# Seven half-width products in place of eight for the SwiGLU down projection, with the weight sums made by GpSimd

## What is computed

```python
def swiglu(h, w_gate_up, w_down):
    g, u = jnp.split(h @ w_gate_up, 2, axis=-1)
    return (jax.nn.silu(g) * u) @ w_down

        x = x + rms_norm(ca, g_mem_post[l])
        h = rms_norm(x, g_ffn_pre[l])
        x = x + rms_norm(swiglu(h, w_gate_up[l], w_down[l]), g_ffn_post[l])
```

## Time and profile before

| | |
|---|---|
| three runs | 1463.42, 1463.74, 1464.24 us, median 1463.74 |
| profiled execution, its own time | 1463.54 us |
| its span in the profile | 1461.7 us |
| PE busy | 1449.6 us (99%) |
| DVE, ACT, POOL busy | 897.9, 616.6, 242.0 us |
| granted clock of PE, mean | 1.000 |

### The profile page before, as it was taken

One profiled execution on the slowest core, in us unless ns is written; L12 is line 12 of the kernel. 1 busy time (PEld: TensorE's weight loads), 2 busy tenths in 40 slices (PEclk: granted clock), 3 DMA queues, 4 the chain that ended last, 5 costly groups with the idle time before them and its releaser, 6 DMA issues.

```text
span 1461.7 us, 21937 instructions
## 1 busy us (share of the span) xinstructions
PE 1449.6 (99%) x8234; PEld 1208.5 (83%) x8234; DVE 897.9 (61%) x1389; ACT 616.6 (42%) x960; POOL 242.0 (17%) x215
## 2 busy tenths in 40 slices
PE   9999999999999999999999899999999999999999
PEld 6888779898899888888888688888888888888787
DVE  6524673566638655455323787747666866767878
ACT  6222775453345222223223542334665433334654
POOL 0200102020020000000000565545522110110000
PEclk9999999999999999999999999999999999999999
DMA  5622103422023665754422122232203333334643
GB/s 177 202 87 93 53 2 122 138 87 87 1 87 116 204 186 185 223 175 155 166 86 90 55 87 90 96 103 87 60 2 87 87 91 110 86 98 132 223 152 122
DMA packets 159251, 164.06 MB, mean 112 GB/s; under 512 B 7357, under 2 KB 134589, under 8 KB 157765
## 3 DMA queue, kind: packets, MB, share of 16 engines
q1 hardware_dynamic: 157268, 159.84, 34.5%
...
q10 hardware_dynamic: 1056, 0.00, 0.0%
...
## 4 chain that ended last, share of the span: by engine, by line
PE 96%; DVE 2%; POOL 1%; DMA 0%; ACT 0%; issue 0%; SPq 0%; DVEq 0%; ACTq 0%; POOLq 0%
PE ps L2259 27%; PE ps L2261 27%; PE ps L2260 27%; PE ps L2696 3%; PE ps L2785 1%; PE ps L2803 1%; PE ps L2886 1%; PE ps L2895 1%; PE ps L2706 1%; PE ps L547 1%; POOL x_t L863 1%; DVE w_lo L2169 1%; DMA raw<-in_w_in 0%; PE ps L2727 0%; PE ps L2954 0%; PE ps L2955 0%
## 5 line engine op out<-in xcount | busy, mean ns | idle before, releaser
L2259 PE MATMUL ps<-a_hi,w_hi 128*128 128x512 f32 (+2 forms) x1576 | 588.6, 373 | 4.9 <-POOL w_lo L811 2.3
L2261 PE MATMUL ps<-a_hi,w_lo 128*128 128x512 f32 (+2 forms) x1576 | 583.3, 370 | 0.0
L2260 PE MATMUL ps<-a_lo,w_hi 128*128 128x512 f32 (+2 forms) x1576 | 583.0, 370 | 0.0
L2259 PEld LDWEIGHTS ps<-a_hi,w_hi 128*128 128x128 f32 (+1 forms) x1576 | 296.2, 188 | 61.3 <-DVE a_lo L1626 4.2
L2261 PEld LDWEIGHTS ps<-a_hi,w_lo 128*128 128x128 f32 (+1 forms) x1576 | 296.2, 188 | 51.6
L2260 PEld LDWEIGHTS ps<-a_lo,w_hi 128*128 128x128 f32 (+1 forms) x1576 | 296.3, 188 | 50.9 <-issue 0.7
L949 ACT ACTIVATE w_hi<-raw 128x2048 fp32r<-128x2048 f32 x105 | 200.8, 1913 | 254.6 <-PE ps L2261 240.2
L1511 DVE TENSOR_TENSOR w_lo<-raw,w_hi 128x2048 fp32r<-128x2048 f32 x85 | 194.6, 2289 | 154.2 <-ACT w_hi L949 153.7
L811 POOL TENSOR_TENSOR w_lo<-raw,w_hi 128x2048 fp32r<-128x2048 f32 x22 | 101.4, 4608 | 435.7 <-ACT w_hi L949 408.0
L2017 DVE TENSOR_TENSOR arena<-ps,rstd 128x512 f32<-128x512 f32 x88 | 59.8, 687 | 137.6 <-PE ps L2261 132.6
L2259 PE MATMUL ps<-w_hi,a_hi 128*128 128x512 f32 x346 | 135.6, 392 | 1.3 <-DVE w_lo L2169 0.9
...
## 6 DMA issues: line engine op xcount, KB each, us to landing
raw<-in_w_gate_up SPq DMA_DIRECT2D x44, 512.0 KB, 5.6
raw<-in_ffn_w_up SPq DMA_DIRECT2D x44, 512.0 KB, 4.7
raw<-in_attn_w_in SPq DMA_DIRECT2D x36, 512.0 KB, 4.5
raw<-in_w_in SPq DMA_DIRECT2D x24, 512.0 KB, 4.7
arena<-in_ffn_w_down SPq DMA_DIRECT2D x24, 512.0 KB, 4.1
...
raw<-in_w_down SPq DMA_DIRECT2D x22, 512.0 KB, 4.4
raw<-in_w_mem_kv SPq DMA_DIRECT2D x16, 512.0 KB, 4.4
```

Source lines behind the costliest of these rows:

```text
L2259: pe.matmul(dst, s_hi, m_hi, start=start, stop=False, skip_group_check=across)
L2260: pe.matmul(dst, s_hi, m_lo, start=False, stop=False, skip_group_check=across)
L2261: return pe.matmul(dst, s_lo, m_hi, start=False, stop=stop, skip_group_check=across)
```

## The change

`ffn_down` becomes seven products of blocks. Both the contraction (each pair of row tiles: rows k=0 and k=1) and the features (two halves of 512) and the tokens (two halves of 256) are cut in two, and seven products of sums of quarters replace eight. Tokens move, 256 at a time. There are 29 steps. Eleven (`DownStep`, one for each pair) hold four of the seven products, with 4 x 4 x 3 = 48 matmuls of 256 tokens. Eighteen (`SingleStep`) are three runs of six steps, each run one product: five steps of two pairs (24 matmuls) and one step of one pair (12 matmuls). The four products share PSUM banks with the single ones: a result is copied out by ACT (`staged_quarter`) or added by DVE (`join_down`) before the run that goes on in its bank.

Weight quarters are summed by POOL, not by DVE: for each of eleven pairs it loads the two row tiles, makes four sums of 128x512, and stores four quarters to `sums_1_dram`. The steps of `ffn_down` read one quarter from `w_down` and three from there, in a ring of four buffers. The sums of activation quarters are POOL's `basis` (two of 128x256 for each pair, as the hidden tiles get ready), three more for a pair are DVE's (`sides`, `fourth_side`). Squares are taken of quarters of the result in the steps 15, 20 and 26 and at the end; the gain moves from ACT's copy into DVE's scaling (L1644 and L1638 become `scalar_tensor_tensor`).

The core of the diff ("..." where lines are left out):

```diff
-    ("ffn_up", 22, 2, 2, "dve"), ("ffn_down", 11, 1, 0, ""),
+    ("ffn_up", 22, 2, 2, "dve"), ("ffn_down", 29, 1, 0, ""),
...
+                self.run, m = (c - PAIRS_K) // 6, (c - PAIRS_K) % 6
+                self.pairs = range(2 * m, min(2 * m + 2, PAIRS_K))
+                self.many = len(self.pairs)
+                self.opens, self.closes = m == 0, m == 5
...
+            def load_down():
+
+                for t in DOWNS:
+                    if t.c < 2:
+                        sp.wait_ge(weights_split, t.g + CREDIT - 1)
+                    elif t.c < 4:
+                        sp.wait_ge(hidden_written, CREDIT + FT)
+                    else:
+                        sp.wait_ge(weights_split, t.g + CREDIT - 3)
+                    if t.c == 0:
+                        sp.wait_ge(rel_moved, SUMS_1_MOVED + 48 * PAIRS_K)
+                    if t.first:
+                        sp.dma_start(t.q[:, 0, :], w_down_1[t.pair, 0][:, 0:512]).then_inc(t.landed, 16)
+                        sp.dma_start(t.q[:, 1:3, :], sums_1_dram[t.pair, :, 0:2, :]).then_inc(t.landed, 16)
+                        sp.dma_start(t.q[:, 3, :], sums_1_dram[t.pair, :, 3, :]).then_inc(t.landed, 16)
+                    else:
+                        def operand(pair):
...
+                                return sums_1_dram[pair, :, 2, :]
+                            return w_down_1[pair, 1].rearrange("p (q n) -> p q n", n=512)[:, 2 - t.run, :]
+                        if t.many == 2:
+                            for j, pair in enumerate(t.pairs):
+                                sp.dma_start(t.q[:, j, :], operand(pair)).then_inc(t.landed, 16)
+                        else:
+                            for half in (slice(0, 256), slice(256, 512)):
+                                sp.dma_start(t.q[:, 0, half], operand(t.pairs[0])[:, half]).then_inc(t.landed, 16)
...
+            def sums_of_quarters(pair):
+
+                b11, b12, b21, b22 = (quarter_set_1[:, n, :] for n in range(4))
+                pool.wait_ge(rel_moved, SUMS_1_MOVED + 48 * pair)
+                for k in range(2):
+                    pool.dma_start(quarter_set_1[:, 2 * k:2 * k + 2, :],
+                                   w_down_1[pair, k].rearrange("p (q n) -> p q n", n=512)).then_inc(rel_moved, 16)
+                pool.wait_ge(rel_moved, SUMS_1_MOVED + 48 * pair + 32)
+                pool.tensor_tensor(b22, b22, b12, ALU.subtract).then_inc(quarter_sums_1, 1)
+                pool.tensor_tensor(b12, b12, b11, ALU.subtract).then_inc(quarter_sums_1, 1)
+                pool.wait_ge(quarter_sums_1, 4 * pair + 1)
+                pool.tensor_tensor(b11, b22, b11, ALU.add).then_inc(quarter_sums_1, 1)
+                pool.wait_ge(quarter_sums_1, 4 * pair + 3)
+                pool.tensor_tensor(b21, b21, b11, ALU.subtract).then_inc(quarter_sums_1, 1)
+                pool.wait_ge(quarter_sums_1, 4 * pair + 4)
+                pool.dma_start(sums_1_dram[pair], quarter_set_1).then_inc(rel_moved, 16)
...
+                sums_of_quarters(pair)
             pool.wait_ge(mask_ready, 3)
-            for _, name, pre in OPENED.values():
-                sum_squares(norms[name])
+            sum_squares(norms["mix_post"])
+            for pair in range(2, 6):
+                sums_of_quarters(pair)
+            sum_squares(norms["mem_post"])
+            for t in DOWNS[:PAIRS_K]:
+                if t.pair < PAIRS_K - 6:
+                    sums_of_quarters(t.pair + 6)
+                basis(t)
...
+            def operands_hi(t):
+
+                end = G[t.up].signal_end
+                act.wait_ge(t.landed, t.landed_at)
+                if t.c < 2:
+                    act.wait_ge(tile_done, end - 2 + 2 * t.c)
+                else:
+                    act.wait_ge(tile_done, end + t.c - 1)
+                act.activation(t.weight(w_hi), t.q[:, 0:t.many, :], ACT.Copy).then_inc(weights_hi, 1)
+
...
+            for t in DOWNS[2:]:
+                operands_hi(t)
+                if t.c + 1 < DOWN_STEPS:
+                    sides_hi(DOWNS[t.c + 1])
+                if t.c == RUNS[0]:
+                    act.wait_ge(sums_stored, 16 * PAIRS_K)
+                    act.wait_ge(rel_moved, SUMS_1_MOVED + 48 * PAIRS_K)
+                    staged_quarter(1, P7_1, y_quarter(0, 0))
+                    staged_quarter(2, P1_1, v_sum)
+                    staged_quarter(3, P5_1, y_quarter(1, 1))
...
+            split_hi(Chunk(G["ffn_down"], 0, 2, DOWN_STEPS - 1))
             act.wait_ge(mask_ready, 10)
...
-            root_of(norms["ffn_post"], ps[:, 4, 0:4])
+            act.wait_ge(post.added, CREDIT + 5)
+            for h in range(2):
+                act.wait_ge(product_done, 5 + 2 * h)
+                act.activation(token_squares(1)[:, 2 * h:2 * h + 2, :], bank_quarter(P1_1)[:, 2 * h:2 * h + 2, :],
+                               ACT.Square).then_inc(post.sq, 1)
+            root_of(post, ps[:, 4, 0:4])
+            act.wait_ge(product_joined, 2)
+            act.activation(y_quarter(0, 0), bank_quarter(P1_1), ACT.Copy).then_inc(post.sq, 1)
             split_hi(Chunk(G["dil_in"], 0, 6, 0))
...
+                    for t in DOWNS[0:3]:
+                        sides(t)
+                    operands_lo(DOWNS[0])
+                    sides_lo(DOWNS[0])
+                    sides_lo(DOWNS[1])
+                    sides(DOWNS[3])
...
+            for t in DOWNS[2:]:
+                if 3 <= t.c < PAIRS_K - 2:
+                    sides(DOWNS[t.c + 2])
+                operands_lo(t)
+                if t.c + 1 < DOWN_STEPS:
+                    sides_lo(DOWNS[t.c + 1])
...
+                if t.first:
+                    fourth_side(t)
+                if t.c == 4:
+                    sums_of_quarters(PAIRS_K - 1)
+                if t.c - RUNS[0] in (1, 2, 3):
+                    join_down(t.c - RUNS[0])
+                elif t.c == RUNS[0] + 5:
+                    add_squares(1, 0, HALVES[1], 0, True)
+                elif t.c == RUNS[1] + 1:
+                    join_down(4)
+                elif t.c == RUNS[1] + 4:
+                    add_squares(2, 1, HALVES[1], 2, False)
+                elif t.c == RUNS[2] + 1:
+                    join_down(5)
...
+            def seven_products_by_feature():
+
+
+                for t in DOWNS:
+                    pe.wait_ge(hidden_split, t.sides_after)
+                    pe.wait_ge(weights_split, t.g + 1 + CREDIT)
...
+                        for a, w, bank in t.products():
+                            if t.c == 0 and bank == P6_1:
+                                pe.wait_ge(freed["dve"], CREDIT + G["ffn_up"].freed_end)
+                            for f in range(4):
+                                cols = slice(f * 128, f * 128 + 128)
+                                last = three(feature_quarter(bank, f), (whi[:, w, cols], wlo[:, w, cols]),
+                                             (hi[:, a:a + 256], lo[:, a:a + 256]), t.c == 0 and f % 2 == 0,
+                                             t.pair == PAIRS_K - 1, across=True)
+                            if t.pair == PAIRS_K - 1 and bank != P6_1:
+                                last.then_inc(product_done, 1)
...
+                        pe.wait_ge(product_staged, (1, 3, 2)[t.run])
+                    ends = t.c == DOWN_STEPS - 1
+                    if ends:
+                        pe.wait_ge(norms["ffn_post"].added, CREDIT + 7)
+                        by_token(square_sum, True, False)
+                    for f in range(4):
+                        cols = slice(f * 128, f * 128 + 128)
+                        for j in range(t.many):
+                            last = three(feature_quarter(t.bank, f), (whi[:, j, cols], wlo[:, j, cols]),
+                                         (hi[:, j, :], lo[:, j, :]), False, t.closes and j == t.many - 1, across=True)
+                        if ends:
...
-                by_token(square_sum, True, False)
-
             def summed(norm, then):
 
-                pe.wait_ge(norm.sq, KT)
-                by_token(squares[:, 3, :], False, True).then_inc(norm.sum, 1)
+                for f in range(4):
+                    pe.wait_ge(norm.sq, 4 + f // 2)
+                    for b in range(2):
+                        last = pe.matmul(ps[:, 4, b:b + 1], token_squares(1)[:, f, b * 128:b * 128 + 128], ones[:, 0:1],
+                                         start=False, stop=f == 3, skip_group_check=True)
+                last.then_inc(norm.sum, 1)
                 stay_clocked(then, 5)
```

More of the change, by code:

```diff
@@ L42, with step_loads, ring_loads, raw_shift @@
 ]
+PAIRS_K = FT // 2
+DOWN_STEPS = 29
+DOWN_RING = 4
+def step_loads(c):
+    return 48 if c < PAIRS_K else 32
+def ring_loads(buffer, until=DOWN_STEPS):
+    return sum(step_loads(c) for c in range(buffer, until, DOWN_RING))
+def raw_shift(slot, chunk0):
+    return ring_loads((slot - chunk0) % 2) - 32 * len(range((slot - chunk0) % 2, DOWN_STEPS, 2))
 class Gemm:
@@ L60, in plan @@
     return gemms, chunk
```

(52 more changed lines are left out.)

335 lines of the change are left out of this document (181 added, 154 removed).

## The result

The changed kernel takes 1475.1 us (median of four, 1474.59 to 1478.46) against 1463.97 before: ratio 1.0081, interval 1.0066 to 1.0095. It is 11 us slower, where 1464.5 was forecast and 1468.5 was the upper end.

What follows compares the result with a forecast made beforehand. TensorE's own work was taken as the bound, PE busy 99% of the span. Terms -8.9 + 1.0 + 3.8 + 2.2 + 2.7 = +0.8 on 1463.54, the median 0.2 above, gave 1464.5 us, range 1460.0 to 1468.5.

Steps and rivals of the forecast that it cites:

- PE's work and the stage: ffn_down: 924 matmuls at 0.1199, 110.8 us, a gain of 8.9; with sums of squares and stalls 115.6, 4.1 less.
- Run ends: ffn_down, behind a step of 12 matmuls: operands come 1.26 us late, at two places, +2.5.
- the chain of 2.7: ffn_down's single steps: rounding and handing on the operands takes 2.7 us, fitting into 2.88 by 0.2.
- The tail: From ffn_down's end to dil_in: +2.2, of which root later +1.2 and copy ahead of the split +1.0.
- the late root: Behind ffn_down: ACT's squares wait for chunk 0's split, root at about 3.6 where it was 2.4, +1.2.
- The bound of 3.2: Upper bound of the wait added behind ffn_down, if dil_in's chunk 0 load lands a microsecond later.
- GpSimd's sums: Eight POOL sums in mem_q's and ffn_up's openings delay DVE's cycle: 3.5, some two falling on nothing, so +2.7.
- a POOL sum costs the chain about 0.44: mem_q's and ffn_up's openings: DVE stretch per POOL sum, from L1626's 0.74 alone and 1.18 beside L863.
- and are stored by about 530, long before step 0: Five pairs' POOL sums from mem_post on are ready well before ffn_down; no term of their own.
- my rival by that rule: Full exclusion in mem_q's and ffn_up's openings: 4.6 to 7.2 in place of 2.7, 1466.4 to 1469.0; chance 0.15.
- The clock: Lower clock level after the longer wait behind ffn_down: with too-late sums, a few in a hundred together.
- The rivals: Faster, sums hidden: 1461.4, chance 0.22. Slower: full exclusion, 1466.4 to 1469.0, 0.15; single steps chain-bound, 1468.3, 0.13.

Runs made afterwards that it cites:

- later_tail: later plus dil_in's first weight chunk loaded earlier and ACT's split of its second chunk ahead of the quarter's copy: 1460.6 us (0.9981).
- later: Changed kernel, all work kept: pairs 2 to 4 wait until mem_q's opening is over, pairs 5 to 10 follow from ffn_up's third turn: 1464.1 us (1.0002).
- ffn_up_early: Changed kernel, all work kept: pairs 2 to 4 wait for mem_q's opening to end, ffn_up's start stays filled, pair 5 loaded at 474: 1471.4 us (1.0054).
- neither: Changed kernel without POOL's four sums per pair and without its loads (but the first pair's) and stores; basis sums stay: 1463.55 us (0.9998).
- no_sums: Changed kernel without POOL's four sums of each pair, its loads and stores kept: 1473.5 us (1.0067).

## Why the prediction was wrong

**PE's work and the stage: right.** 924 matmuls at 0.12; 115.6 forecast, 115.66 where nothing disturbs. Run ends 1.24 for 1.26; step 1 0.98 for 1.2; the sum of squares 0.81 for 0.96; single steps without a wait, so the chain of 2.7 did fit into 2.88; the last sums in step 4 0.1. Only step 2's late load (0 to 0.75) had no term.

**The tail: right mechanism, too small.** 2.2 forecast, 2.5 to 3.7 measured. The two terms are confirmed by later_tail, whose tail is 2.7 shorter than later's. The mis-sized term is the late root, 2.07 in the changed kernel where 1.2 was forecast; the copy was 0.91 for 1.0. The second half of `dil_in`'s chunk 0 was 5.2 us under way and landed at the end of the stage, not 0.7 ahead. The bound of 3.2 was for that, and three runs lie clearly above it (3.4 in ffn_up_early, 3.55 in neither, 3.7 in no_sums).

**GpSimd's sums: two steps failed.** The first is "a POOL sum costs the chain about 0.44", and with it that only the eight sums in the two openings count. For those eight it held: 1.2 in `mem_q`'s and 1.1 in `ffn_up`'s opening, 2.3 for the 2.7. But it was taken from L1626 beside L863, where every second operation of DVE (L1638) reads PSUM and keeps its 0.68 us. Where both engines have operations of two SBUF inputs back to back, each of DVE's waits about 1.0. And pair 3, which my own spacing of 16 us put at 337 to 342, had no term, although L1606 ahead of PE's sum of squares has only 0.35 us of slack. That missing term measured 4.15 of `mem_q`'s 5.35, the clock's 1.6 included. The Trainium skill's rule ("SBUF — State Buffer", Who interferes with whom: the second of the two fully blocks) comes nearer here than my 0.44: full exclusion would make a turn 1.29 + 0.69 = 1.98, the rows show 1.7. But my rival by that rule, 4.6 to 7.2 for both openings, was again without pair 3.

The second is in the same paragraph: "and are stored by about 530, long before step 0". I asked of POOL's transfers only whether they are done in time, and gave no price to what they delay. `ffn_up`'s window (476 to 688) had a DMA share of 0.61 on the mean, and I checked the rate of `ffn_down` only. At `ffn_up`'s start the chunks had just been caught up; before, the chunk at 498.05 had been waited for 7.65 us by ACT, with PE not yet idle. That is the row that says there is no room. This cost 7.2 us of the 14.5, and nothing of mine covered it.

**The clock** had been given to a few in a hundred, behind `ffn_down`. There it fell too, to 0.50 between 824 and 827.5, in time that PE waits through anyway. It cost where it was not looked for: 1.6 us behind `mem_q`'s wait, 2.1 behind `ffn_up`'s.

**The rivals.** None of them was it. The forecast of "no change" looks like what the change gives without these two costs (neither: 1463.55; later: 1464.1), but that is luck: without its 2.7 for the sums the forecast's own terms give 1461.8, and the tail, at 3.55 for 2.2, makes up most of the difference.

What stays open: in the changed kernel the store is 3.1 us longer under way and the chunk behind it 2.2, by the rows above, but no run lets SP load the chunk without waiting for the store, so what that order alone costs was not tried apart.
